# The front of a hybrid decode step: page columns loaded in two halves, constants in two parts, products in another order

## The reference, cut to what matters

```
mod = silu(c) @ w_ada + b_ada                      # adaLN: shift, scale, gate of 9 conditions
h   = modulate(rms_norm(x, g), shift1, scale1)     # goes into the input projection w_in

def compress(k, pe, w1, w2):                       # NSA: key pages and value pages, each with its weights
    idx    = arange(nc)[:, None] * 16 + arange(32)[None, :]
    blocks = k[:, idx] + pe[None, None, :, None, :]
    flat   = blocks...reshape(B, nc, 2, 32 * 64)
    return gelu(flat @ w1) @ w2
```

## Time and profile before

| | us |
|---|---|
| three runs | 761.25, 763.62, 762.53 (median 762.53) |
| the profiled execution, its own time | 761.43 |
| its span, first to last instruction | 759.7 |
| TensorE busy | 692.7 (91% of the span) |
| VectorE / ScalarE / GpSimd busy | 288.3 / 171.9 / 84.4 |
| TensorE's granted clock over the span | 0.990 of full |
| DMA | 236.07 MB, mean 311 GB/s |

### The profile page before, as it was taken

The page is one execution under the profiler, slowest core; times in us unless marked ns, Lnnn a source line. Parts: engine busy times, 40 slices in busy tenths (PEclk is TensorE's granted clock), DMA queues, the critical chain, the costliest instruction groups (busy, mean ns, idle before and its releaser), DMA issues.

```text
span 759.7 us, 12425 instructions
## 1 busy us (share of the span) xinstructions
PE 692.7 (91%) x4598; PEld 384.4 (51%) x4598; DVE 288.3 (38%) x897; ACT 171.9 (23%) x410; POOL 84.4 (11%) x127
## 2 busy tenths in 40 slices
PE   0999999999999999899998999999999997878884
PEld 0766666558665665454555676574333322222332
DVE  1653333610102787665531232486411211111246
ACT  0214344112101564332241001421110101100102
POOL 3001000003400343110000000011212121112000
PEclk9999999999999999999999999999999999999997
DMA  9999986717344963999999991518999999999961
GB/s 301 427 405 358 407 310 230 304 51 274 112 166 167 363 248 114 328 353 373 392 391 386 421 421 50 232 60 314 420 418 419 417 420 416 420 419 419 420 217 69
DMA packets 57939, 236.07 MB, mean 311 GB/s; under 512 B 9108, under 2 KB 16029, under 8 KB 42836
## 3 DMA queue, kind: packets, MB, share of 16 engines
q1 hardware_dynamic: 49700, 218.41, 73.4%
q0 software_dynamic: 6592, 15.39, 5.6%
q10 hardware_dynamic: 1584, 1.44, 0.6%
HBM read 230.52 MB, written 19.14 MB: 329 GB/s over the span
## 4 chain that ended last, share of the span: by engine, by line
PE 68%; SPq 13%; DMA 10%; DVE 5%; issue 3%; ACT 1%; POOLq 1%; POOL 0%; DVEq 0%
PE bank L611 14%; SPq L466 7%; PE bank L1138 6%; PE bank L1030 5%; PE bank L1014 5%; DMA arena<-in_w_eout 4%; SPq L485 4%; PE bank L658 3%; PE bank L542 3%; PE bank L738 2%; PE bank L1160 2%; PE bank L563 2%; PE bank L962 2%; PE bank L572 2%; PE bank L875 2%
## 5 line engine op out<-in xcount | busy, mean ns | idle before, releaser
L1138 PE MATMUL bank<-arena 128*32 128x512 f32 (+1 forms) x928 | 116.4, 603 | 15.1 <-DMA arena<-in_w_ein 13.9
L611 PE MATMUL bank<-arena 128*128 128x320 f32 x384 | 106.6, 433 | 1.0 <-DVE arena L1518 1.0
L611 PEld LDWEIGHTS bank<-arena 128*128 128x128 f32 x384 | 71.6, 189 | 35.5 <-issue 6.4
L1138 PEld LDWEIGHTS bank<-arena 128*32 128x32 f32 (+1 forms) x928 | 32.4, 114 | 87.5 <-issue 66.7
L1160 PE MATMUL bank<-arena 128*32 128x512 f32 (+1 forms) x464 | 58.3, 595 | 7.0 <-DMA arena<-in_w_eout 6.6
L1994 DVE COPY arena<-bank 128x512 f32<-128x512 f32 x14 | 9.7, 691 | 106.5 <-PE bank L1101 106.5
L1455 ACT ACTIVATE arena<-bank 128x256 f32<-128x256 f32 x16 | 6.2, 386 | 153.6 <-PE bank L1138 153.6
L563 PE MATMUL bank<-arena 128*128 128x256 f32 x64 | 17.2, 425 | 20.3 <-DMA arena<-in_cmp_pages 20.3
L1160 PEld LDWEIGHTS bank<-arena 128*32 128x32 f32 (+1 forms) x464 | 15.7, 112 | 38.6 <-issue 30.0
L1270 ACT ACTIVATE arena<-bank 32x320 f32<-32x320 f32 x60 | 25.8, 430 | 41.7 <-PE bank L611 41.1
L1030 PE MATMUL bank<-arena 128*128 128x320 f32 x128 | 35.0, 432 | 0.0
(11 more groups left out here) (413 smaller groups left out, 1008.0 us busy)
## 6 DMA issues: line engine op xcount, KB each, us to landing
arena<-in_w_ein SPq DMA_DIRECT2D x52, 1024.0 KB, 25.2
arena<-in_w_eout SPq DMA_DIRECT2D x26, 1024.0 KB, 26.7
arena<-in_w_ada SPq DMA_DIRECT2D x12, 2048.0 KB, 11.6
arena<-in_w_in SPq DMA_DIRECT2D x10, 2048.0 KB, 9.1
arena<-in_k_pages SPq DMA_DIRECT2D x64, 320.0 KB, 6.1
arena<-in_v_pages SPq DMA_DIRECT2D x64, 320.0 KB, 8.9
arena<-in_w_ein SPq DMA_DIRECT2D x3, 4096.0 KB, 22.1
arena<-in_w_eout SPq DMA_DIRECT2D x3, 2048.0 KB, 13.6
```

The source lines that it names most:

```text
L611: m = mm(banks[c % 4][:, 0:N], ring[q][:, k, P * (c % 4):P * (c % 4 + 1)], hT[:, k, :], start=(k == 0), stop=(k == KD - 1))
L1138: m = mm(banks[2 + p % 2][r:r + n, :], xeT[p % 2][:, k, r:r + n], wi2[p % 3][:, e, k, :], start=(k == 0), stop=(k == KD - 1))
```

## The change: what it does

- Each of the three queues first reads the numbers of all of its first pages into registers, then issues the DMAs of the 128 key columns of all of them (rows of 512 bytes), and later those of the 128 value columns, under semaphores of their own. SyncE issues the value weights and the vectors between the two.
- The constants are laid out anew, with the identity, the ones and the half mask first. This part (258 of 2238 columns) is loaded behind `xT`, the rest behind the ring's tile w0.
- TensorE starts with eight matmuls of 128x512 from the key weights into bank 7, which nobody reads.
- TensorE's order: the key products, the loop at 630, `cmp_odd` and `cmp_second` of the values, the folding at 639, the square sums, `ada(0)`, the first half of the values' `cmp_first`, `ada(1)`, `turn_ada(0)`, its second half, `ada(2)`, `turn_ada(1)`, `ada(3)`, `turn_ada(2)`, `turn_ada(3)`. VectorE and ScalarE follow: VectorE copies the rows of 630 out ahead of `block_differences(0, 1)`, and ScalarE does the first Gelu before the square root, the squares after the first copy.
- The semaphore of the vectors and that of the output are merged into that of the page table.

The diff, without the merged semaphore of the output and a count of constants that follows from the split:

```diff
@@ -56,22 +56,25 @@
 LAST = PAIRS - 1
 ALLP = PAIRS + EXTRA // 2
 NOWHERE = 1000000.0
-
-
-C_ID, C_TRI, C_R, C_NEW = 0, 128, 512, 640
+WARM = 8
+
+
+C_ID, C_ONE, C_HALF = 0, 128, 256
+C_FIRST = C_HALF + 2
+C_TRI = C_FIRST
+C_R = C_TRI + 384
+C_NEW = C_R + 128
 C_WIN = C_NEW + 4 * NS
 C_CADD = C_WIN + 8
 C_C01 = C_CADD + 2 * NCMPP
 C_IDX = C_C01 + 2 * NCMPP
-C_ONE = C_IDX + 16
-C_COS = C_ONE + 128
+C_COS = C_IDX + 16
 C_SIN = C_COS + N
 C_LT = C_SIN + N
 C_E = C_LT + 128
 C_PUT = C_E + E
 C_ROOM = C_PUT + E
-C_HALF = C_ROOM + E
-C_ROW = C_HALF + 2
+C_ROW = C_ROOM + E
 C_PLACE = C_ROW + 128
 C_TOK = C_PLACE + 128
 C_ALL = C_TOK + 8
@@ -256,11 +259,13 @@
         idx = cst[:, C_IDX:C_IDX + 16]
 
 
-        s_pg, s_vec, s_x, s_cst = sem("page_numbers_loaded"), sem("vectors_loaded"), sem("x_loaded"), sem("constants_loaded")
+        s_pg = sem("page_numbers_loaded_then_vectors_loaded_then_y_written")
+        s_x, s_cst = sem("x_loaded"), sem("constants_loaded")
         s_w = [sem(f"weight_tile_loaded{k}") for k in range(3)]
         s_w1 = sem("cmp_value_weights_loaded")
-        s_w1k, s_xc = sem("cmp_key_weights_loaded"), sem("cmp_pages_loaded")
-        s_xcp = sem("cmp_pages_loaded_by_gpsimd")
+        s_w1k, s_xc = sem("cmp_key_weights_loaded"), sem("cmp_key_pages_then_second_half_loaded")
+        s_xcp, s_xv = sem("cmp_key_pages_loaded_by_gpsimd"), sem("cmp_value_pages_loaded")
+        s_xvp = sem("cmp_value_pages_loaded_by_gpsimd")
         s_k = [sem(f"keys_loaded{g}") for g in range(2)]
         s_v = [sem(f"values_loaded{g}") for g in range(3)] + [sem("values_loaded3_then_second_half_of_out_weights")]
         s_wbr = [sem(f"branch_weights_loaded{h}") for h in range(2)]
@@ -372,11 +377,16 @@
                         sp.dma_start(dst[b][:, p * 640:(p + 1) * 640],
                                      src[bass.ds(ids[i % 3][b][p], 1), :, :].rearrange("o p n -> (o p) n")).then_inc(s, 16)
 
-            cmp_pages_of(0, 0, 11)
-            sp.dma_start(vecs, vec).then_inc(s_vec, 16)
+            first_pages = [page_of(j // PAGES, j % PAGES) for j in range(11)]
+            for j, pg in enumerate(first_pages):
+                sp.dma_start(xc[:, j, 0:P], cmp_pages[bass.ds(pg, 1), :, 0:P].rearrange("o p n -> (o p) n")).then_inc(s_xc, 16)
             sp.dma_start(w1_sb[1], w1[:, 1]).then_inc(s_w1, 16)
+            sp.dma_start(vecs, vec).then_inc(s_pg, 16)
+            for j, pg in enumerate(first_pages):
+                sp.dma_start(xc[:, j, P:2 * P], cmp_pages[bass.ds(pg, 1), :, P:2 * P].rearrange("o p n -> (o p) n"))\
+                    .then_inc(s_xv, 16)
             sp.dma_start(xT, x_t).then_inc(s_x, 16)
-            sp.dma_start(cst, consts).then_inc(s_cst, 16)
+            sp.dma_start(cst[:, 0:C_FIRST], consts[:, 0:C_FIRST]).then_inc(s_cst, 16)
             def tile_in(n):
 
                 kind, tile = RING[n]
@@ -386,6 +396,8 @@
 
             for n, (kind, tile) in ((n, entry) for n, entry in enumerate(RING[:-1]) if entry):
                 tile_in(n)
+                if kind == "w" and tile == 0:
+                    sp.dma_start(cst[:, C_FIRST:], consts[:, C_FIRST:]).then_inc(s_cst, 16)
                 if kind == "w" and tile == 1:
                     sp.wait_ge(s_cAB, 4)
                 if kind == "w" and 1 <= tile <= 3:
@@ -554,8 +566,12 @@
 
             def cmp_odd(half, v):
 
-                te.wait_ge(s_xc, 352 + 512 * half)
-                te.wait_ge(s_xcp, 160)
+                if half or v == 0:
+                    te.wait_ge(s_xc, 352 + 512 * half)
+                    te.wait_ge(s_xcp, 160)
+                else:
+                    te.wait_ge(s_xv, 352)
+                    te.wait_ge(s_xvp, 160)
                 te.wait_ge(s_bd, 8 if half else 2 + 3 * v)
                 for t in range(8):
                     c = P * v + 16 * t
@@ -613,35 +629,38 @@
                 m.then_inc(s_proj, 1)
 
             te.wait_ge(s_w1k, 16)
+            for f in range(WARM):
+                mm(banks[7][:, :], w1_sb[0][:, f, :], w1_sb[0][:, 0:4, :], start=True, stop=True)
             cmp_odd(0, 0)
             cmp_second(0, 0)
             cmp_first(0, 0, 0, 8)
+            te.wait_ge(s_w1, 16)
+            te.wait_ge(s_pg, 32)
+            for t in range(8):
+                for j in range(4):
+                    v, u = j // 2, 2 * t + j % 2
+                    m = mm(banks[4][32 * j:32 * j + 1, 0:P], pe[:, v, u:u + 1], w1_sb[v][:, u, :], start=(t == 0), stop=(t == 7))
+            m.then_inc(s_pb, 1)
+            cmp_odd(0, 1)
+            cmp_second(0, 1)
             te.wait_ge(s_cst, 16)
+            te.wait_ge(s_pbv, 1)
+            mm(banks[4][:, 256:258], hp, cst[:, C_HALF:C_HALF + 2], start=True, stop=True).then_inc(s_pb, 1)
             te.wait_ge(s_sq, 1)
             for k in range(KD):
                 m = mm(banks[5][:, 0:N], ones, sq[:, k, :], start=(k == 0), stop=(k == KD - 1))
             m.then_inc(s_ss, 1)
             te.wait_ge(s_silu, 1)
             ada(0)
-            te.wait_ge(s_w1, 16)
-            for t in range(8):
-                for j in range(4):
-                    v, u = j // 2, 2 * t + j % 2
-                    m = mm(banks[4][32 * j:32 * j + 1, 0:P], pe[:, v, u:u + 1], w1_sb[v][:, u, :], start=(t == 0), stop=(t == 7))
-            m.then_inc(s_pb, 1)
+            cmp_first(0, 1, 0, 4)
             ada(1)
             turn_ada(0)
-            cmp_odd(0, 1)
+            cmp_first(0, 1, 4, 8)
             ada(2)
             turn_ada(1)
-            cmp_second(0, 1)
-            te.wait_ge(s_pbv, 1)
-            mm(banks[4][:, 256:258], hp, cst[:, C_HALF:C_HALF + 2], start=True, stop=True).then_inc(s_pb, 1)
             ada(3)
             turn_ada(2)
-            cmp_first(0, 1, 0, 4)
             turn_ada(3)
-            cmp_first(0, 1, 4, 8)
             for t in range(4):
                 for c in range(4 * t, 4 * t + 4):
                     chunk(c)
@@ -1017,7 +1036,7 @@
             te.wait_ge(s_she, 1)
             for c in range(KD):
                 if c == 4:
-                    te.wait_ge(s_cst, 32)
+                    te.wait_ge(s_cst, 48)
                     for t in range(4):
                         mm(banks[7][0:RT, 36 * t:36 * (t + 1)], cond_hot[:, RT * t:RT * (t + 1)], shift_logits, start=True, stop=True)
                 if c % 4 == 0:
@@ -1221,20 +1240,6 @@
                 part = rstd[64:P, :] if n == 2 else rstd
                 act(part, part, ACT.Sqrt).then_inc(s_rms, 1)
 
-            def cmp_pages_of(first, last):
-                for j in range(first, last):
-                    pg = sc.value_load(page_row[0:1, j:j + 1], min_val=0, max_val=NPHYS - 1)
-                    sc.dma_start(xc[:, j, :], cmp_pages[bass.ds(pg, 1), :, :].rearrange("o p n -> (o p) n"))\
-                        .then_inc(s_xc, 16)
-
-            sc.wait_ge(s_pg, 16)
-            cmp_pages_of(11, 22)
-            sc.wait_ge(s_vec, 16)
-            sc.wait_ge(s_bd, 1)
-            act(condS[:, :, 0:NC], cT, ACT.Silu).then_inc(s_silu, 1)
-            sc.wait_ge(s_x, 16)
-            act(sq, xT, ACT.Square).then_inc(s_sq, 1)
-
             def cmp_odd_out(half, v):
                 n = 2 * half + v
                 sc.wait_ge(s_cAB, 4 * half + 2 * v + 1)
@@ -1538,7 +1556,10 @@
 
             def block_differences(half, v):
 
-                if v == 0:
+                if half == 0 and v == 1:
+                    ve.wait_ge(s_xv, 352)
+                    ve.wait_ge(s_xvp, 160)
+                elif v == 0:
                     ve.wait_ge(s_xc, 352 + 512 * half)
                     ve.wait_ge(s_xcp, 160)
                     if half:
@@ -1596,23 +1617,23 @@
             block_differences(0, 0)
             ve.wait_ge(s_w1, 16)
             weight_sum(1)
+            ve.wait_ge(s_pb, 1)
+            for j in range(4):
+                m = ve.tensor_copy(hp[32 * j:32 * j + 1, :], banks[4][32 * j:32 * j + 1, 0:P])
+            m.then_inc(s_pbv, 1)
             block_differences(0, 1)
             cmp_sums(0, 0)
+            ve.wait_ge(s_pb, 2)
+            ve.tensor_copy(peb, banks[4][:, 256:258]).then_inc(s_pbv, 1)
             ve.wait_ge(s_x, 16)
             ve.wait_ge(s_ss, 1)
             root(banks[5][:, 0:N], 1)
             ada_rows(0)
             link(normed(sq))
             ada_rows(1)
-            ve.wait_ge(s_pb, 1)
-            for j in range(4):
-                m = ve.tensor_copy(hp[32 * j:32 * j + 1, :], banks[4][32 * j:32 * j + 1, 0:P])
-            m.then_inc(s_pbv, 1)
             ada_mod(0)
             ada_rows(2)
             ada_mod(1)
-            ve.wait_ge(s_pb, 2)
-            ve.tensor_copy(peb, banks[4][:, 256:258]).then_inc(s_pbv, 1)
             ada_rows(3)
             ada_mod(2)
             ada_mod(3)
@@ -1621,6 +1642,8 @@
             modulated(hT, sq, scl[:, 0], mod[:, 0:8, :])
             cmp_sums(0, 1)
```

(11 more changed lines are left out.)

21 lines of the change are left out of this document (17 added, 4 removed).

## The result

| | before | after |
|---|---|---|
| median, us | 762.74 | 769.49 (768.56 to 769.77) |
| ratio of the two, with 95% interval | | 1.0073 [1.0052, 1.0093] |
| the profiled execution / its span | 761.43 / 759.7 | 769.38 / 767.7 |
| first key product starts / takes | 20.27 / 6.04 | 20.37 / 5.40 |
| `chunk(0)` starts | 61.12 | 65.00 |

A forecast was written before the change was run, and what follows sets the result against it. First-data landing and TensorE's list behind it set chunk(0)'s start; DMA is second. Reordering costs 3.7 us, clock returns 2.4, landing 2.0: 0.8 earlier, taken from the 762.53 median, gives 761.7 us; range 759.9 to 765.3.

The forecast's parts named there:

- the list: TensorE's work from the key landing to chunk(0), added up piece by piece to 42.3 us.
- the keys need 7.3 us: landed at 18.0: Key loading: data flow from 10.7 us, 2.10 MB at an estimated 286 GB/s, so the last key half lands at 18.0.
- the upper bound: Key landing at 14.30 + 5.7 = 20.0 us, if the last GpSimd page takes as long as before.
- rival 3: Key tail delayed by turns with the value weights' long rows: landing 20.0, clock falls, chunk(0) 2.9 us later; chance 0.17.
- Between keeping the clock and losing 1.7 I take keeping it: Pause of some 2 us between unread products and keys: the clock stays at 2.4 GHz, so 1.7 us are not lost.
- Stands bare: Modulation between the last turn and chunk(0): 2.75 us uncovered, where half of cmp_first covered 1.9 before.
- the other pause: TensorE's idle time between the unread products and the key landing, some 2 us; a clock fall there priced at 1.7 us.
- The waits of 0.8, 0.3, 0.8 and 2.75: TensorE idle before cmp_second of the values, before ada(3), between the last two turns, and before chunk(0), in us.
- T + 42.3: Start of chunk(0): 42.3 us after the last key half lands at time T, at full clock; 60.3 for T = 18.0.
- all have cover: Loads behind the keys land before TensorE wants them; a3 and the values have the least cover, 2.3 and 2.1 us.
- passed on one for one: From the input projection on: a shift of chunk(0)'s start, put at 0.8 us earlier, reaches the kernel's end in full.

The follow-up runs named there:

- e1: Changed kernel with the value weights issued behind SyncE's value halves; 769.71 us, ratio 1.0090 to the kernel before.
- e5: Changed kernel with each key half issued right behind its own register load instead of after all the loads; 765.51 us, ratio 1.0038 to the kernel before.
- e6: Changed kernel without the eight unread products; 769.11 us, ratio 1.0088 to the kernel before.
- e9: Changed kernel with 13 unread products instead of eight; 766.91 us, ratio 1.0035 to the kernel before.
- e11: e8 with GpSimd's 7 MB of output writes held until weight tile w1 has landed; 760.59 us, ratio 0.9949 to the kernel before.
- e4: Changed kernel with the second half of the values' cmp_first moved back behind turn_ada(3); 772.26 us, ratio 1.0120 to the kernel before.
- e10: Changed kernel with three unread 128x512 products in the wait between turn_ada(3) and chunk(0); 768.20 us, ratio 1.0054 to the kernel before.
- e8: Changed kernel with key halves issued load by load, a0 and other loads ahead of SyncE's value halves, and a new compute order; 761.51 us, ratio 0.9977.
- e7: e4 with the constants loaded whole behind xT instead of in two parts; 767.56 us, ratio 1.0062 to the kernel before.
- e12: The changed kernel run again, unaltered, beside other kernels on the same chip; 767.95 us, ratio 1.0066 to the kernel before.
- e3: Changed kernel with pages loaded whole, register load and DMA in turn as before; 769.30 us, ratio 1.0058 to the kernel before.

## Why the prediction was wrong, step by step

The forecast was 761.7, close to no change, with a range up to 765.3; measured is 769.49. It put `chunk(0)` at 60.3, and it started at 65.0: 2.3 us of that are the landing, 1.8 the slow first product and some 0.6 the list behind it. Another 1.7 came behind `chunk(0)`, from a fall of the clock that the sum did not have.

- **Wrong: "the keys need 7.3 us: landed at 18.0".** The last landed at 20.3. The rate was about right (286 estimated, 273 by the row measured) and two queues were done at 18.6. The step that failed is the end of the stream: I let the keys run alone to the end, but from 14.2 on the value halves and the value weights share the engines, and GpSimd's last half, behind its backlog, took 6.1 us. That I gave as the upper bound and as rival 3; its mechanism, the long rows of the value weights, is only 0.5 us of it (e1). The backlog that stands when the last key halves are issued, and that the bunched register loads make, is the cause (e5: 2.7 us). How much of the rest the value halves of the other queues take was not tried by itself. Half the bytes, started 5 us later, arrive at the same time.
- **Wrong: "Between keeping the clock and losing 1.7 I take keeping it".** It fell (0.63 at 20 to 24.6). Since the keys were late, the pause was 4.6 us and not 2, so the unread products gave nothing in place of 2.4: the first product took 5.40 us with them and 5.53 without (e6), and 3.72 where they ran on to 1.15 us before it (e9). The 0.6 us against the 6.04 of before is no more than such products differ by from one profile to the next. In e11, with a pause of 2.1 us, the product took 3.72, so for a pause of the forecast's length the choice held.
- **Missed: the clock behind the bare wait.** "Stands bare" was priced at its own length of 2.75 (2.77 measured). It also lets the clock fall, 14.88 - 13.20 = 1.7 us, a term that the sum put at nothing, though it had the same price for the other pause. e4 and e10 show it. It is not all to be won back: w1, landing at 87.2, would have held TensorE up from 86.0 on.
- **Right: the list.** The waits of 0.8, 0.3, 0.8 and 2.75 came as 0.66, 0.32, 0.75 and 2.77. T + 42.3 plus 1.8 for the slow first product gives 64.4 at T = 20.3; measured is 65.0.
- **Right in this kernel, but by luck: "all have cover".** I listed a0 to a3 and w0 and stopped. w1 had 0.5 us left of 15.8. In the new order each `ada` is done 5 to 10 us later, the ring moves on later, and its tiles meet GpSimd's writes. Issuing w1 early is not enough, though: in e5 and e8 it goes out at 55.4 and 54.3, as in the kernel before, and takes 27.3 and 27.1 us. There a4, ahead of it in SyncE's queue, lands at 68.5 and 64.6, after the first writes have been issued (61.2 and 60.9); in the kernel before it landed at 60.1, ahead of them (62.2). e4, e7 and e11 show the price on both sides.
- **Right: passed on one for one**, from the end of the first three chunks to 314 us, and in e12 to within 0.5 us up to the end.

The sum as measured, in the profiles: start of the first product +0.1, first product -0.6, waits in the list 4.9 against 1.6 = +3.3, and 1.1 more in the pieces between them, since a product's end no longer lies under the next one's start where a wait parts them, and several products take 0.1 us longer: `chunk(0)` +3.9. The clock in the first chunks +1.7. Together 5.6, beside 6.75 in the medians of the first comparison and 6.0 between the spans in e12. Of what remains the runs show only that half-clock stretches later in the program come in some executions and not in others: the one at 516 us is there in the changed kernel and in e9 and not in e12. How much of it is due to the change stays open.

## What to carry to other kernels

When a load is split so that its first half lands early, check when the first byte starts, not when the last DMA is issued: here ten register loads put in front cost all that halving the bytes gave, and interleaving them brought the first product forward by 3.3 us. Price a wait that loses its cover twice, once for its length and once for the clock behind it, and put filler work into the wait itself, up to its end; a gain there shows only if the next load is in time (e10). And when an order is changed, follow the buffers that it frees late down to the next large transfer on the same DMA engines.

## What the runs showed of the hardware

- Rows of 512 bytes moved 246 GB/s at a share of 0.90; 1 KB rows 342 at 1.06, and rows of 8 KB and more 426 at 1.02.
- Register loads in a row took as long as ones with a DMA between: the first DMA went out at 8.57, where 3.08 + 10 x 0.56 gives 8.7.
- GpSimd's last 64 KB key half, issued at the same time, took 6.1 us behind a backlog (changed kernel) and 2.7 without one (e5). A 2 MB tile took 27.1 us beside GpSimd's writes and 15.5 with these held back (e8, e11).
- The granted clock fell after or during pauses of 4.6 us and of 2.8 us, the latter in every profile that has it (the changed kernel both times, e1, e3, e5, e6, e9); with the pause filled (e10) it did not. Pauses of 1.1 to 2.1 us ahead of the first product (e5, e8, e11) left it full.
